# Two transformer blocks at 256 tokens: RMS norms applied after the product instead of before it

## What is computed

```
norm(x, g) = x * rsqrt(mean(x*x, over D) + 1e-6) * g        # one factor per token, one weight per feature
h  = mixer 1(x)                                             # delta rule + attention, 16 heads, own input norm
h  = h + mix @ w_out
h  = h + square(relu(norm(h, mlp_norm) @ w_up)) @ w_down    # width 8192
h  = norm(h, final_norm)                                    # end of block 1
p  = norm(h, layer_norm[0]) @ mla_w_in                      # block 2, layer 0: c_q, c_kv, k_rope, gate
c_q, c_kv = norm(c_q, ..), norm(c_kv, ..)                   # ranks 512
h  = h + (attention(c_q @ .., c_kv @ .., rope) * silu(gate)) @ mla_w_out
p  = norm(h, layer_norm[1]) @ swa_w_in                      # layer 1: q, k, v, gate; window of 128, sinks
h  = h + (attention(rope(q), rope(k), v) * silu(gate)) @ swa_w_out
return norm(h, final_norm_2)
```

## Time and profile before

| | us |
|---|---|
| three runs | 3291.08, 3296.51, 3298.01 (median 3296.51) |
| the profiled execution, its own time | 3298.15 |
| its span, first to last instruction | 3296.4 |
| TensorE busy | 3067.9 (93%) |
| VectorE busy | 1856.2 (56%) |
| ScalarE busy | 1496.6 (45%) |
| GpSimd busy | 16.2 (0%) |
| mean granted clock of TensorE | 0.969 |

### The profile page before, as it was taken

The page is one execution under the profiler, slowest core; times in us unless marked ns, Lnnn a source line. Parts: engine busy times, 40 slices in busy tenths (PEclk is TensorE's granted clock), DMA queues, the critical chain, the costliest instruction groups (busy, mean ns, idle before and its releaser), DMA issues.

```text
span 3296.4 us, 58168 instructions
## 1 busy us (share of the span) xinstructions
PE 3067.9 (93%) x21345; PEld 2818.0 (85%) x21345; DVE 1856.2 (56%) x3093; ACT 1496.6 (45%) x2669; POOL 16.2 (0%) x26
## 2 busy tenths in 40 slices
PE   4999999999999899999899999999779999788888
PEld 4999999999999799998788888888678988778877
DVE  4655665566566444445565656565445555455654
ACT  4555555555555344443443434333444443444443
POOL 0000000000000000000000000000000000000000
PEclk8999999999999899999999999999889999899999
DMA  4333333333333255556355555555234435333334
GB/s 159 121 119 121 122 121 119 121 121 127 113 122 121 95 183 182 176 191 198 127 183 182 183 183 185 184 181 182 97 115 141 151 117 184 103 109 108 115 121 153
DMA packets 128018, 472.69 MB, mean 143 GB/s; under 512 B 14256, under 2 KB 14256, under 8 KB 127504
## 3 DMA queue, kind: packets, MB, share of 16 engines
q1 hardware_dynamic: 125136, 457.23, 41.4%
q0 software_dynamic: 2752, 13.65, 1.3%
HBM read 468.59 MB, written 2.24 MB: 143 GB/s over the span
## 4 chain that ended last, share of the span: by engine, by line
PE 80%; DVE 9%; ACT 6%; issue 4%; DMA 1%; ACTq 0%; DVEq 0%; POOL 0%; POOLq 0%
PE bank L275 20%; PE bank L277 13%; PE bank L278 12%; PE bank L279 12%; PE bank L276 10%; DVE w_lo L251 2%; PE bank L625 2%; ACT w_hi L245 2%; PE bank L611 2%; PE bank L341 1%; PE bank L621 1%; PE bank L560 1%; DVE norm_v L360 1%; DVE mix_kT L1421 1%; DVE u L365 1%
## 5 line engine op out<-in xcount | busy, mean ns | idle before, releaser
L251 DVE TENSOR_TENSOR w_lo<-raw,w_hi 128x1024 fp32r<-128x1024 f32 x866 | 1034.1, 1220 | 414.2 <-ACT w_hi L245 404.4
L245 ACT ACTIVATE w_hi<-raw 128x1024 fp32r<-128x1024 f32 x866 | 895.6, 1053 | 465.2 <-PE bank L276 393.1
L277 PE MATMUL bank<-u,w_hi 128*128 128x256 f32 (+1 forms) x3328 | 1022.1, 307 | 45.4 <-DVE u L365 26.5
L278 PE MATMUL bank<-u,w_hi 128*128 128x256 f32 (+1 forms) x3328 | 958.0, 288 | 0.0
L279 PE MATMUL bank<-u,w_lo 128*128 128x256 f32 (+1 forms) x3328 | 956.5, 287 | 0.0
L277 PEld LDWEIGHTS bank<-u,w_hi 128*128 128x128 f32 x3328 | 640.4, 192 | 70.4 <-issue 30.8
L278 PEld LDWEIGHTS bank<-u,w_hi 128*128 128x128 f32 x3328 | 639.9, 192 | 4.7
L279 PEld LDWEIGHTS bank<-u,w_lo 128*128 128x128 f32 x3328 | 638.5, 192 | 0.0
L275 PE MATMUL bank<-ya,w_hi 128*128 128x512 f32 x1536 | 549.0, 401 | 15.1 <-DVE ya L1667 10.9
L276 PE MATMUL bank<-ya,w_lo 128*128 128x256 f32 x1536 | 435.0, 283 | 0.0
L275 PE MATMUL bank<-u,w_hi 128*128 128x512 f32 x1024 | 360.8, 396 | 13.7 <-DVE u L365 13.7
(11 more groups left out here) (309 smaller groups left out, 3756.1 us busy)
## 6 DMA issues: line engine op xcount, KB each, us to landing
raw<-in_stream SPq DMA_DIRECT2D x868, 512.0 KB, 3.3
mix_row<-rows POOLq DMA_DIRECT2D x16, 408.0 KB, 4.0
xT<-in_xT POOLq DMA_DIRECT2D x1, 2176.0 KB, 16.6
consts<-in_consts POOLq DMA_DIRECT2D x1, 2146.0 KB, 10.7
h<-in_xT POOLq DMA_DIRECT2D x1, 2048.0 KB, 9.8
out_dram<-h SPq DMA_DIRECT2D x1, 2048.0 KB, 6.3
vecs<-in_vecs POOLq DMA_DIRECT2D x1, 166.5 KB, 10.8
rows<-scalars_out POOLq DMA_DIRECT2D x1, 136.0 KB, 3.1
```

The lines of the kernel that those rows point to most:

```text
L245: act.activation(w_hi[:, slot], raw[:, slot], ACT.Copy).then_inc(hi_ready, 1)
L251: dve.tensor_tensor(w_lo[:, slot], raw[:, slot], w_hi[:, slot].bitcast(F32), ALU.subtract).then_inc(lo_ready, 1)
L277: pe.matmul(o, a, x[:, 0], start=first, stop=False)
L278: pe.matmul(o, a, x[:, 1], start=False, stop=False)
```

## The change

In a norm the token's factor can be applied after a product, since it is the same for all features. From `out` on, the products run on `u` = h * weight, split while the stage before still runs: ScalarE's `high_part` (a copy scaled by the weight) and VectorE's `low_part` follow each residual tile. GpSimd squares each finished tile of `h` and adds it to a running sum (two instructions a tile; four after the last `down`, where two norms follow one another: the second norm's sum of squares is that of h * final_norm, and both factors are combined in `both_rs`). TensorE sums over features once, with one ones-matmul (`total`, two after the last `down`), placed four product steps ahead of the end of the next stage's first tile; ScalarE takes Ln and Exp (`root_of_total`).

The factor is applied where the results leave PSUM. In `up`: VectorE multiplies relu by the factor, ScalarE squares and then copies (one ScalarE instruction more a tile). In `mla_in`: VectorE evacuates with the factor instead of ScalarE, and multiplies `h` by final_norm and factor beside it. For gates of `mla` and `swa` VectorE first writes gate * factor and frees the bank, ScalarE takes tanh of that, VectorE forms the gate from both. In `swa` q and k stay unscaled and the cosines and sines are scaled; v is scaled at evacuation.

The barriers before stages become a wait for all tiles but the last (two), and for the last only ahead of the first tile's last step. The norms of c_q and c_kv move beside `mla_in` (c_kv's ends beside the first slab of `mla`), the turn of k_rope into `mla`, the k turns into `swa_kv`, the v transposes into the first `swa` tile. The sines' arguments are computed by GpSimd during the first `up` (39 instructions; the sines by ScalarE during the last `down`), and GpSimd's load of the positions stands behind its first sums. The final output is scaled in place tile by tile and stored in four parts instead of one. The first norm (line 319 on, with 272 tokens) stays as it was.

```diff
@@ products, full_tile
             for k in range(HALF_KT):
+                if last and ready is not None and k == HALF_KT - ready[2]:
+                    pe.wait_ge(sem(ready[0]), ready[1])
+                if last and midway is not None and k == HALF_KT - 4:
+                    midway()
                 mm = product(pe, slot, k, o, x(k if first else HALF_KT + k), first and k == 0,
                              last and k == HALF_KT - 1)
             mm.then_inc(slab_used, 1)
...
+            if ready is not None:
+                pe.wait_ge(sem(ready[0]), ready[1] - 1)
...
@@ new helpers
+        def high_part(act, norm, k):
+            await_tile(act, NORM_AFTER[norm], k)
+            act.activation(u[:, k, 0, META:], h[:, k], ACT.Copy, scale=gain(norm, k)).then_inc(sem("u hi"), 1)
+        def low_part(dve, norm, k):
+            dve.wait_ge(sem("u hi"), norm * KT + k + 1)
+            dve.scalar_tensor_tensor(out=u[:, k, 1, META:], in0=h[:, k], scalar=gain(norm, k),
+                                     in1=u[:, k, 0, META:].bitcast(F32), op0=ALU.mult,
+                                     op1=ALU.subtract).then_inc(sem("u lo"), 1)
+        def sum_squares(gp, norm):
...
+            for k in range(KT):
+                await_tile(gp, NORM_AFTER[norm], k)
...
+                gp.tensor_tensor(late_sq[:, k % 2], h[:, k], h[:, k], ALU.mult).then_inc(sem("square"), 1)
+                gp.wait_ge(sem("square"), n + 1)
...
+                gp.tensor_tensor(late_sum[:, 0], late_sum[:, 0], late_sq[:, k % 2], ALU.add).then_inc(sem("sum"), 1)
+                if norm == 1:
+                    gp.wait_ge(sem("sum"), n + 1)
+                    gp.tensor_scalar(late_sq[:, k % 2], late_sq[:, k % 2], gains[:, 1, k:k + 1], None,
+                                     ALU.mult).then_inc(sem("square gained"), 1)
...
+                    gp.tensor_tensor(late_sum[:, 1], late_sum[:, 1], late_sq[:, k % 2], ALU.add).then_inc(
+                        sem("sum of gained"), 1)
+        def total(pe, norm):
+            pe.wait_ge(sem("sum"), (norm + 1) * KT)
+            pe.matmul(bank[2][:, 0:SEQ], const("ones"), late_sum[:, 0], start=True,
+                      stop=True).then_inc(sem("total"), 1)
+            if norm == 1:
+                pe.wait_ge(sem("sum of gained"), KT)
+                pe.matmul(bank[2][:, SEQ:2 * SEQ], const("ones"), late_sum[:, 1], start=True,
...
+            act.activation(late_ln[:], bank[2][:, 0:SEQ], ACT.Ln, scale=1.0 / D,
+                           bias=const("eps")).then_inc(sem("total ln"), 1)
+            act.wait_ge(sem("total ln"), norm + 1 + (norm > 1))
+            act.activation(late_rs[:], late_ln[:], ACT.Exp, scale=-0.5).then_inc(sem("rs"), 1)
@@ SyncE, GpSimd
-            sp.wait_ge(sem("norm done"), 6)
-            sp.dma_start(out, h[:]).then_inc(sem("out written"), 16)
-            sp.wait_ge(sem("out written"), 16)
+            for part in range(4):
+                ks = slice(part * KT // 4, (part + 1) * KT // 4)
+                sp.wait_ge(sem("scaled"), KT + (part + 1) * KT // 4)
+                sp.dma_start(out[:, ks], h[:, ks]).then_inc(sem("out written"), 16)
+            sp.wait_ge(sem("out written"), 64)
-            await_slab(gp, "mla_in", -1)
+            sum_squares(gp, 0)
             gp.dma_start(pos_i[:], positions_in.partition_broadcast(P).rearrange("p a n -> p (a n)")).then_inc(
                 sem("positions in"), 16)
...
+            for norm in range(1, 4):
+                sum_squares(gp, norm)
@@ TensorE
+            matrix("out", mx, ("mix lo", KT, 1))
             for q in range(QUARTERS):
-                matrix(f"up{q}", u_seq)
-                pe.wait_ge(sem("hidden lo"), (q + 1) * KT)
-                matrix(f"down{q}", ya)
-            norm_pe(pe, 2, SEQ)
-            norm_pe(pe, 3, SEQ)
-            pe.wait_ge(sem("norm lo"), 3 * KT)
+                matrix(f"up{q}", u_seq, ("u lo", KT, 1), None if q else lambda: total(pe, 0))
+                matrix(f"down{q}", ya, ("hidden lo", (q + 1) * KT, 1))
...
+                full_tile(pe, "mla_in", t, u_seq, SEQ, 2 * t, ready=("u lo", 2 * KT, 1),
+                          midway=None if t else lambda: total(pe, 1))
+                if t == RT + 1 or t == MLA_IN_TILES - 1:
+                    g = int(t > RT + 1)
...
                     pe.wait_ge(lo_ready, m + 1)
+                    if not off and j == 1:
+                        pe.wait_ge(sem("c lo"), 2 * RT)
...
-            pe.wait_ge(sem("c lo"), 2 * RT)
-            pe.wait_ge(sem("rotated"), 1)
+            pe.wait_ge(sem("c lo"), RT)
...
-            pe.wait_ge(sem("mla lo"), HEADS // 2)
-            matrix("mla_out", ya)
-            norm_pe(pe, 4, SEQ)
...
+                full_tile(pe, "swa_kv", t, u_seq, SEQ, 2 * t, ready=("u lo", 3 * KT, 1),
+                          midway=None if t else lambda: total(pe, 2))
+                if 1 <= t <= 4:
+                    await_tile(pe, "swa_kv", t - 1)
+                    pe.wait_ge(sem("rotated"), t + SWA_K_TURNS - 2)
...
-            pe.wait_ge(sem("swa lo"), KT)
-            matrix("swa_out", ya)
-            norm_pe(pe, 5, SEQ)
+            matrix("swa_out", ya, ("swa lo", KT, 1))
+            total(pe, 3)
@@ ScalarE
+            def matrix_split(phase, norm, turns=()):
+                for t in range(KT):
+                    ahead(phase, 2 * t + 2)
+                    if t and norm < 3:
+                        high_part(act, norm, t - 1)
...
+                    act.wait_ge(sem("hidden lo"), n - 2)
+                act.wait_ge(sem("hidden r"), n)
+                act.activation(sum_t[:, s], hid_v[:, s], ACT.Square).then_inc(sem("hidden v"), 1)
+                act.wait_ge(sem("hidden v"), n)
+                k = bass.ts(s if i is None else i * 2 + s, 1)
+                act.activation(ya_x[:, k, 0, :], sum_t[:, s, None, :], ACT.Copy).then_inc(sem("hidden hi"), 1)
...
+                    act.wait_ge(sem("gained"), 2)
+                    act.activation(late_ln[:], late_sq[:, 0], ACT.Ln, scale=1.0 / D,
+                                   bias=const("eps")).then_inc(sem("total ln"), 1)
+                    act.wait_ge(sem("total ln"), 3)
+                    act.activation(late_sq[:, 1], late_ln[:], ACT.Exp, scale=-0.5).then_inc(sem("rs of gained"), 1)
...
-                    await_slab(act, "mla", 8 * off + 5 + 2 * s, i, 8)
-                    if s:
-                        b, turn = tile_no("mla", 8 * off + 6, i, 8)
-                        act.wait_ge(tile_free[b], turn + 2)
-                    b, _ = tile_no("mla", 6 + s)
-                    act.activation(gate_t[:], proj[b][:, 0:SEQ], ACT.Tanh, scale=0.5).then_inc(
...
+                    b, turn = tile_no("mla", 8 * off + 6 + s, i, 8)
+                    act.wait_ge(tile_free[b], turn + 2)
+                    act.activation(gate_t[:], gate_v[:], ACT.Tanh, scale=0.5).then_inc(sem("mla tanh"), 1)
...
-                                await_slab(act, "swa", 4 * tile + 3, i, 16)
-                                b, _ = tile_no("swa", 2 * tile + 1)
-                                act.activation(s_th[:], proj[b][:, 0:SEQ], ACT.Tanh, scale=0.5).then_inc(
+                                b, turn = tile_no("swa", 2 * tile + 1, i, 8)
+                                act.wait_ge(tile_free[b], turn + 2)
+                                act.activation(s_th[:], s_gv[:], ACT.Tanh, scale=0.5).then_inc(
                                     sem("swa tanh"), 1)
@@ VectorE
+                for t in range(KT):
+                    ahead(phase, 2 * t + 2)
+                    if t:
...
+                    dve.tensor_tensor(o, proj[b][:, 0:SEQ], o, ALU.add).then_inc(sem("half added"), 1)
+                    dve.wait_ge(sem("half added"), residuals[0] * KT + t + 1)
+                    dve.tensor_tensor(o, proj[b][:, SEQ:2 * SEQ], o, ALU.add).then_inc(tile_free[b], 1)
...
+                dve.scalar_tensor_tensor(out=hid_v[:, s], in0=relu_t[:, s], scalar=0.0, in1=late_rs[:],
+                                         op0=ALU.max, op1=ALU.mult).then_inc(sem("hidden r"), 1)
+                dve.wait_ge(sem("hidden hi"), first + (q * KT + s + 1))
+                t = bass.ts(first + s, 1)
+                dve.tensor_tensor(ya_x[:, t, 1, :], sum_t[:, s, None, :], ya_x[:, t, 0, :].bitcast(F32),
+                                  ALU.subtract).then_inc(sem("hidden lo"), 1)
...
+                if t == 0:
+                    dve.wait_ge(sem("rs"), 2)
+                    dve.tensor_tensor(late_sq[:, 0], late_rs[:], late_rs[:], ALU.mult).then_inc(sem("gained"), 1)
...
+                    dve.wait_ge(sem("rs of gained"), 1)
+                    dve.tensor_tensor(both_rs[:], late_rs[:], late_sq[:, 1], ALU.mult).then_inc(sem("both rs"), 1)
+                    dve.wait_ge(sem("both rs"), 1)
+                await_slab(dve, "mla_in", 2 * t + 1)
+                b, _ = tile_no("mla_in", t)
```

(33 more changed lines are left out.)

427 lines of the change are left out of this document (248 added, 179 removed).

## The result

The changed kernel takes 3168.69 us (median of four runs, 3167.83 to 3169.43), the one before 3296.32 on the same chip: a ratio of 0.9614, 95% interval 0.9602 to 0.9626, 127.6 us less. The forecast was 3168. The profiled execution took 3168.02, its span 3166.3 (before 3296.4); TensorE is busy for 95% of it, at a mean granted clock of 0.980 (before 0.969).

What follows compares the result with a forecast made beforehand. TensorE, busy for 93% of the span, was taken as the bound, so only its stops and slowed clock counted. 3298.15 less gains of 151.8 plus costs of 22 gave 3168.4, taken as 3168 us; range 3146 to 3200.

Steps and rivals of the forecast that it cites:

- terms 1 to 6: Five stage boundaries from out to swa and the kernel's end: TensorE's stops there shrink or close, gain 119.8 us.
- the clock 11: Behind five boundaries: TensorE's restarts at the low clock go, 5 x 2.2 = 11 us gained.
- The end: Term 6, behind the last product: 14.2 us remain of 22.9, gain 8.7.
- The barriers: TensorE's waits for the last split before stages (10.9 for four together, 2.5, 2.4, 1.7) go: gain 17.5 us.
- The gate in mla: In mla VectorE's first instruction frees the bank, shortening TensorE's wait by 0.45 us a pair: gain 3.5 us.
- Swa: In swa tanh waits for VectorE's gate * factor, 16 steps x 1.13 = 18 us cost; bounds 0 and 28.
- GpSimd: GpSimd's sums take 0.6 us an instruction and may get in VectorE's way: cost 3 us, possibly nothing to 47.
- Rival C: GpSimd holds VectorE up, above all after the last down with four instructions a tile: 3180 to 3212 us; chance 0.14.
- Rival E: GpSimd's queue falls behind the tiles, from 1.4 us an instruction on; slower than before, 3448 at 4 us; chance 0.04.
- Rival D: The up loop becomes the bound through ScalarE's added instruction: 3183 us at 0.25 a tile, 3199 at 0.5; chance 0.10.
- The cost of 1 us: In up, one more ScalarE instruction adds 0.45 us to a loop with 0.45 to 0.56 room: 1 us for 64 tiles.
- A second sign: Outside swa, no window with a clock near 0.5 after 1500 us.

Runs made afterwards that it cites:

- one_store: The changed kernel with the output stored in one part behind the last scaling instead of in four parts: 3171.9 us.
- barriers_back: The changed kernel with TensorE's waits for all 16 split tiles put back ahead of out, each down, mla_out and swa_out: 3194.3 us.
- no_square_sums: The changed kernel with GpSimd squaring and summing only the last of 16 tiles in each of the four norms: 3169.1 us.
- six_gpsimd_ops: The changed kernel with six GpSimd instructions a tile instead of four in the last down: 3185.2 us.
- two_squares_in_up: The changed kernel with ScalarE's square in each up tile done twice: 3186.5 us.

## Why the prediction was right

**The boundaries** (terms 1 to 6) carried the result. Their six terms gave 119.8 and the clock 11; the table's rows for them agree within 3 us each but for down3 (41.4 for 35.7). There the whole stop of 39.6 us is gone, since its two ones-matmuls stand in mla_in now; 1.7 was the low clock behind down3's barrier, and the 3 us of cost never arose. The end, 8.7 forecast and 8.8 measured, also bears out the four stores (one_store).

**The barriers**, 17.5 by the waits, gave 11.6 us at the downs, 3.0 ahead of mla_out and 1.8 ahead of swa_out. At out the 2.4 us were given back at once: TensorE reached out's second tile sooner and there waited 5.8 us for w_lo, since VectorE stood at the load of h, which is issued only when merge has ended. The step forgot what was late next. On the other side the prediction put the low clock behind such short stops at nothing, and it was there before the change: the first tiles of down1, down2, down3 and mla_out give 1.6, 1.6, 1.6 and 1.9, some 6.7 us of gain that no term holds. The table shows 1.5 less of it, because down2's other tiles had run at the faster pace. barriers_back agrees: with stops of 3.3 us for 2.7, the first tiles of the downs lose 7 us.

**The gate in mla**, 3.5 forecast, gave 1.9.

**Swa** is the term that was mis-sized: 18 forecast, 24.8 measured. The mechanism was right in place and price for a single step: 1.13 forecast, 0.9 to 1.1 measured between like steps. What failed is the choice of the value between the bounds: I left the low-clock stretches to the upper one (28). Of the 25.8 us in 14 steps, 7 more low stretches at 19.57 - 17.97 = 1.6 make 11, and the handover 14 x 1.04 the other 15. The waits themselves grew by what was forecast: most of those for att_probs went from 2.27 us to 3.38 (the means of 2.1 and 2.7 have short ones in them), and the four for swa_neg_sink, which the prediction did not look at, by 3.8 together.

**GpSimd**, 3 forecast: nothing measured for the sums (no_square_sums), though two of the sentences under it were wrong. "I take 0.6" holds only where VectorE is silent (0.61, 0.72); beside w_lo it is 1.5 and 1.6. And `w_lo`'s mean did rise in the last down, which I had named as a sign that the prediction is wrong. It was no such sign: VectorE lost 0.9 us a tile of the 1.9 of room that the same text had worked out. Rival C's price, (4x - 1.9) x 16, was too high because it let all four instructions block VectorE for their full length, while 0.9 us a tile was lost to all of them, with two instructions a tile as with four. The Trainium skill ("SBUF — State Buffer", section "Who interferes with whom") says that a VectorE instruction with two SBUF inputs contends with a GpSimd instruction that reads SBUF, and calls the shared ports an exclusive lock. The trace agrees that the two hold each other up: the low part doubles from 0.48 to 0.96 and GpSimd's square goes from 0.61 to 1.52. It does not bear out a full block each time, which is what the prediction made of it: each w_lo of 1.22 us lost only 0.21 beside instructions of over 0.6. The estimate of 0.6 to 0.7 us from the Trainium skill ("GPSIMD Engine Reference", section 3.1) fits the instructions with VectorE silent.

**Rival E** was nearer than its chance says: GpSimd had 0.55 us left in the last down, and two instructions more already cost 16.5 us (six_gpsimd_ops). Crossing that line costs the lateness of 16 tiles once, not 130 us; to end slower than before would have taken far more.

**Rival D**: the up loop stayed at TensorE's pace, 89.6 us for each of up1 to up3, with 0.2 us a tile left. In up0 five tiles took 5.65, 5.82, 5.84, 5.71 and 5.71 us for 5.6, 0.7 us in all. They are as long in no_square_sums, so it is not the sums. Four of the five lie beside GpSimd's 39 instructions, but so do the four tiles before them, which took 5.6; that those instructions are the cause is not shown. The cost of 1 us was right in effect, and two_squares_in_up shows that the line was close.

So the mechanisms held, and that the sum came out within 1 us is luck. Against the forecast's column, the table's rows that came out better sum to 12.4 us (above all down3 5.7, mla_out 2.5, the start 1.8, down0 to down2 1.7) and those that came out worse to 12.2 (above all swa 8.2, out 1.9, mla 1.6). The 1.8 us at the start lie ahead of out in code that didn't change, where the kernels with the same code differ by 2.6. A second sign did not come either: the granted clock was to stay up outside swa after 1500 us, but in the first tile of mla_out it was 0.86, behind a wait of 1.95 us for att_probs at the end of mla.

## What to carry to other kernels

When a factor is moved behind a product, look up where the added instruction stands in each engine's order, not how long it takes: here moving one tanh from in front of a weight split to behind it gave 30 us. Where a stop of TensorE is short and repeated, count the low clock that may follow, not the wait alone. And when a barrier is taken away, ask what is late next (here a load), and split that too.

## What the runs showed of the hardware

GpSimd and VectorE lengthen each other: GpSimd's 256-element instructions from 0.61 and 0.72 to 1.52 and 1.60 us, VectorE's low part from 0.48 to 0.96, w_lo from 1.22 to 1.43 in the mean. TensorE's clock after a stop of 3 us is not the same each time: after the four stops ahead of down in barriers_back it was 1.00, 0.50, 0.50 and 0.66 in the 5 us that followed; after stops of 2.65, 2.77, 2.75 and 2.75 us in the kernel before, it stayed up once and fell three times. At a granted clock of 1.00 the same tile of products takes 5.55 us in one stage and 5.65 in another, and which of the two differs between profiled executions whose code is the same there; the cause is open. Whether the steps of swa with the copies of own keys (20.2 us before, up to 22.5 with the tanh behind w_hi) have a remedy of their own was not tried.
